# Two gate products per token become one, and the gates of the second half of the keys come back in two parts

## The reference, cut to what matters

```python
q = (hf @ w_q).reshape(T, PEER_HEADS, 2, PEER_DQ // 2)
s = jnp.einsum('thpd,hpnd->thpn', q, sub_keys)
sc, idx = lax.top_k(s, PEER_TOPK)
...
top_sc, pos = lax.top_k(cand, PEER_TOPK)
eidx = jnp.take_along_axis(cidx, pos, axis=-1)
gate = jax.nn.softmax(top_sc.astype(jnp.float32), axis=-1).astype(h.dtype)
...
act = jax.nn.gelu(jnp.einsum('thkd,td->thk', u_tab[eb], hb), approximate=False)
return jnp.einsum('thk,thkd->td', gb * act, v_tab[eb])
```

## Time and profile before

| | |
|---|---|
| median of 3 runs (lowest, highest) | 3542.27 us (3540.53, 3545.55) |
| the profiled execution | 3543.44 us |
| its span, first to last instruction | 3541.7 us |
| TensorE busy | 3341.8 us, 94% |
| VectorE busy | 2201.1 us, 62% |
| ScalarE busy | 905.8 us, 26% |
| GpSimd busy | 1880.8 us, 53% |
| DMA, mean over the span | 178 GB/s |

### The profile page before, as it was taken

One profiled execution on the slowest core, in us unless ns is written; L12 is line 12 of the kernel. 1 busy time (PEld: TensorE's weight loads), 2 busy tenths in 40 slices (PEclk: granted clock), 3 DMA queues, 4 the chain that ended last, 5 costly groups with the idle time before them and its releaser, 6 DMA issues.

```text
span 3541.7 us, 39029 instructions
## 1 busy us (share of the span) xinstructions
PE 3341.8 (94%) x14292; PEld 2517.4 (71%) x14292; DVE 2201.1 (62%) x3653; ACT 905.8 (26%) x1952; POOL 1880.8 (53%) x1072
## 2 busy tenths in 40 slices
PE   8999999999999999999999999997899988996898
PEld 5779778886857888688776677766899655663433
DVE  5764443337674333589367767899655896566765
ACT  4564431112174111201123413222211221111111
POOL 3544269997104999698775472222577333342420
PEclk9999999999999999999999999999755999998999
DMA  4430022222302222234312127777622899999996
GB/s 161 166 130 1 24 86 102 97 107 83 131 36 72 95 95 95 83 110 143 104 72 95 37 89 300 279 267 279 220 86 103 333 364 417 381 412 375 384 417 268
DMA packets 117764, 628.72 MB, mean 178 GB/s; under 512 B 12889, under 2 KB 13017, under 8 KB 62041
## 3 DMA queue, kind: packets, MB, share of 16 engines
q1 hardware_dynamic: 72496, 343.07, 26.3%
q0 software_dynamic: 36864, 268.45, 19.4%
q10 hardware_dynamic: 8232, 14.95, 1.1%
HBM read 607.55 MB, written 18.87 MB: 177 GB/s over the span
## 4 chain that ended last, share of the span: by engine, by line
PE 72%; DVE 11%; DMA 10%; issue 3%; ACT 2%; POOL 1%; DVEq 0%; ACTq 0%; POOLq 0%; SPq 0%
PE bank L1447 13%; PE bank L1448 13%; PE bank L1449 13%; PE bank L2017 6%; PE bank L2032 6%; PE bank L2044 6%; DMA residual<-in_peer_ut 5%; DMA residual<-in_peer_vd 3%; DVE arena L3549 1%; PE bank L1893 1%; PE bank L1875 1%; PE bank L1761 1%; DVE squares L3381 1%; PE bank L1394 1%; PE bank L1639 1%
## 5 line engine op out<-in xcount | busy, mean ns | idle before, releaser
L1449 PE MATMUL bank<-split_arena 128*128 128x512 f32 x1776 | 696.3, 392 | 0.0
L1279 POOL DMA_INDIRECT arena<-in_peer_uv,rstd x181 | 261.8, 1446 | 624.3 <-DVE weight_ring L3561 325.3
L1186 POOL TENSOR_TENSOR split_arena<-weight_ring,ones 128x1024 fp32r<-128x1024 f32 x204 | 505.1, 2476 | 155.1 <-PE bank L1449 99.2
L1447 PE MATMUL bank<-split_arena 128*128 128x512 f32 x1392 | 546.6, 393 | 5.4 <-DVE split_normed L2908 2.5
L1448 PE MATMUL bank<-split_arena 128*128 128x512 f32 x1392 | 542.5, 390 | 0.0
L2017 PE MATMUL bank<-normed,residual 128*128 128x256 f32 x2048 | 483.3, 392 | 55.1 <-ACT arena L2659 37.1
L1188 POOL TENSOR_TENSOR split_arena<-weight_ring,split_arena 128x1024 fp32r<-128x1024 f32 x204 | 520.1, 2550 | 16.0
L2032 PE MATMUL bank<-residual,arena 128*128 128x512 f32 x1024 | 468.7, 604 | 47.3 <-DVE arena L3537 41.4
L2017 PEld LDWEIGHTS bank<-normed,residual 128*128 128x128 f32 x2048 | 395.9, 196 | 162.0 <-issue 59.8
L2032 PEld LDWEIGHTS bank<-residual,arena 128*128 128x128 f32 x1024 | 190.4, 192 | 288.2 <-issue 238.6
L1449 PEld LDWEIGHTS bank<-split_arena 128*128 128x128 f32 x1776 | 334.4, 188 | 73.1
(11 more groups left out here) (508 smaller groups left out, 5476.9 us busy)
## 6 DMA issues: line engine op xcount, KB each, us to landing
residual<-in_peer_ut SPq DMA_DIRECT2D x128, 512.0 KB, 7.5
residual<-in_peer_vd SPq DMA_DIRECT2D x128, 512.0 KB, 11.0
weight_ring<-in_w_up SPq DMA_DIRECT2D x32, 1024.0 KB, 4.8
weight_ring<-in_w_down SPq DMA_DIRECT2D x32, 1024.0 KB, 4.8
weight_ring<-in_w_in SPq DMA_DIRECT2D x32, 1024.0 KB, 4.9
weight_ring<-in_ada_w SPq DMA_DIRECT2D x24, 1024.0 KB, 4.8
weight_ring<-in_w_in_a SPq DMA_DIRECT2D x12, 1024.0 KB, 6.6
weight_ring<-in_w_out SPq DMA_DIRECT2D x12, 1024.0 KB, 6.9
```

What stands on the lines that cost most here:

```text
L1186: pool.tensor_tensor(hi, part, bc_mid(ones[:], DT), ALU.mult).then_inc(split_hi, 1)
L1279: pool.indirect_dma_start(row_places[i][0], None, a["peer_uv"], bass.IndirectOffsetOnAxis(ap=experts[n][:, c:c + 1], axis=0)).then_inc(row ...
L1447: pe.matmul(psum[t.bank][:], hi, a_hi[k], start=first, stop=False)
L1449: return pe.matmul(psum[t.bank][:], hi, a_lo[k], start=False, stop=last)
```

## The change

- The product of a token is one of 128x128 instead of two of 128x64; the eight tokens of a step lie four in each of the two banks.
- Of the eight second one-hots of a step, VectorE makes six in one instruction, without the gate; ScalarE multiplies them by the gate (`scale_ones`, six instructions); GpSimd makes two, with the gate.
- ScalarE copies the second half from both banks in two instructions, and VectorE multiplies the first half from both banks in two, after ScalarE's copies (`gate_read`).
- The stored gates come back in two parts of 32 second keys: 64 loads of 128 KB with eight places instead of 32 of 256 KB with four. The first 40 loads are issued one behind each item's load from item 132 on; the 32 multiplications of the first part stand in the steps of items 131 to 162; the other 32 stand in 4 back steps.
- Rows per stage: 64, 24, 114, 2, 52 instead of 64, 10, 120, 2, 60.

```diff
--- before.py
+++ after.py
@@ -60,7 +60,10 @@
 WHALF = NKEY // 2
 GTOK = 8
 NGATE = DENSE // GTOK
-LOADS = 4
+LOADS = 8
+BACKS = 2
+BACK_J = WHALF // BACKS
+POOL_HOT = 2
 RAWS = 4
 RING8 = 8
 PIECES = 8
@@ -571,6 +574,8 @@
         STEPS += [("item", n) for n in range(WHALF, 3 * WHALF)]
         BACK_AT = len(STEPS)
         STEPS += [("back", i) for i in range(NGATE // LOADS)]
+        BACK_ITEM = WHALF + WHALF + 4
+        back_at = {MIX_AT + WHALF + 3 + q: q for q in range(NGATE)}
         LAST_AT = len(STEPS)
         STEPS += [("item", n) for n in range(3 * WHALF, 4 * WHALF)]
 
@@ -783,7 +788,7 @@
         one_first = [k.rearrange("p (t i) -> p t i", i=NKEY) for k in keys_t]
         one_second = [x.rearrange("p (t j) -> p t j", j=NKEY) for x in (h_tok[:, 2, :], h_tok[:, 3, :])]
         gate_out = [work_a, work_b]
-        gate_back = [k[:, i * SEQ:(i + 1) * SEQ] for k in keys_t for i in range(2)]
+        gate_back = [k[:, i * UNIT_N:(i + 1) * UNIT_N] for k in keys_t for i in range(4)]
         index_t = [masks[:, 3 * i:3 * i + 3, :] for i in range(2)]
         TAIL = W_AT + DENSE * WHALF
         iota_key = arena[:, TAIL:TAIL + NKEY]
@@ -905,6 +910,8 @@
         turn_in = sem("dense_gates_normalized")
         vector_hot = sem("vector_one_hot_ready")
         pool_hot = sem("pool_one_hot_ready")
+        scaled_hot = sem("one_hot_scaled")
+        gate_read = sem("gate_banks_copied")
         gate_stored = [sem(f"gate_half_stored{i}") for i in range(2)]
         gate_landed = [sem(f"gate_half_landed{i}") for i in range(LOADS)]
         gate_used = sem("gate_half_used")
@@ -979,7 +986,7 @@
 
         step_us = [6.1 if s < 35 else 3.6 if s < G_AT else 3.0 if s < MIX_AT else 3.5 for s in range(len(STEPS))]
         row_step = []
-        for a0, a1, rows in ((3, G_AT, 64), (G_AT, MIX_AT, 10), (MIX_AT, BACK_AT, 120), (BACK_AT, LAST_AT, 2), (LAST_AT, LAST_AT + 58, 60)):
+        for a0, a1, rows in ((3, G_AT, 64), (G_AT, MIX_AT, 24), (MIX_AT, BACK_AT, 114), (BACK_AT, LAST_AT, 2), (LAST_AT, LAST_AT + 58, 52)):
             total, at = sum(step_us[a0:a1]), 0
             ends = list(itertools.accumulate(step_us[a0:a1]))
             for i in range(rows):
@@ -1080,15 +1087,17 @@
                     sp.wait_ge(item_done, n - RAWS + 1)
                 sp.dma_start(raws[n % RAWS], a["peer_vd" if value else "peer_ut"][m]).then_inc(raw_landed[n % RAWS], 16)
 
-            def load_gates(q):
-
-                if q == 0:
+            def load_gates(n):
+
+                part, q = divmod(n, NGATE)
+                if n == 0:
                     full(sp, gate_tiles[NGATE - 1][0])
                     for x in gate_stored:
                         sp.wait_ge(x, 16 * NGATE // 2)
-                if q >= LOADS:
-                    sp.wait_ge(gate_used, q - LOADS + 1)
-                sp.dma_start(gate_back[q % LOADS], weights_dram[q]).then_inc(gate_landed[q % LOADS], 16)
+                if n >= LOADS:
+                    sp.wait_ge(gate_used, n - LOADS + 1)
+                sp.dma_start(gate_back[n % LOADS], weights_dram[q][:, part * BACK_J * GTOK:(part + 1) * BACK_J * GTOK]).then_inc(
+                    gate_landed[n % LOADS], 16)
 
             for n in range(len(ITEMS)):
                 load_item(n)
@@ -1099,11 +1108,10 @@
                 elif n == 16:
                     sp.wait_ge(half_done, 2 * (rest_units[2].u + 1))
                     sp.dma_start(y_flat[:, D:3 * D], first_units[PH - 1].src).then_inc(held_landed[0], 16)
-                elif n == 2 * WHALF:
-                    for q in range(LOADS):
-                        load_gates(q)
+                elif BACK_ITEM <= n < BACK_ITEM + NGATE + LOADS:
+                    load_gates(n - BACK_ITEM)
                 elif n == 3 * WHALF + RAWS - 1:
-                    for q in range(LOADS, NGATE):
+                    for q in range(NGATE + LOADS, BACKS * NGATE):
                         load_gates(q)
                     sp.dma_start(H[:, :, :], x_dram).then_inc(x_back, 16)
             for n in range(TT):
@@ -1288,7 +1296,7 @@
                 if q == 0:
                     for x in index_tiles:
                         have(pool, x)
-                for x in range(GTOK // 2, GTOK):
+                for x in range(GTOK - POOL_HOT, GTOK):
                     at = GTOK * t + x
                     m = pool.tensor_scalar(one_second[q % 2][:, x, :], iota_key, index_t[b][:, 1, at:at + 1],
                                            index_t[b][:, 2, at:at + 1], ALU.is_equal, ALU.mult)
@@ -2023,10 +2031,10 @@
                 if m == 0:
                     for t in v_tiles:
                         free(pe, t)
-                    for t, _ in gate_tiles[NGATE - 2:]:
+                    for t in gate_tiles[NGATE - 2] + gate_tiles[NGATE - 1]:
                         have(pe, t)
                 elif m == WHALF:
-                    pe.wait_ge(gate_used, NGATE)
+                    pe.wait_ge(gate_used, BACKS * NGATE)
                 for b in range(2):
                     for c in range(2):
                         x = pe.matmul(psum[2 * b + c][:], blk(weights[:, m % WHALF, :], b), raws[n % RAWS][:, 512 * c:512 * (c + 1)],
@@ -2037,12 +2045,13 @@
 
                 pe.wait_ge(vector_hot, q + 1)
                 pe.wait_ge(pool_hot, q + 1)
+                pe.wait_ge(scaled_hot, q + 1)
                 for t in gate_tiles[q]:
                     free(pe, t)
                 for x in range(GTOK):
-                    for half, t in enumerate(gate_tiles[q]):
-                        m = pe.matmul(psum[t.bank][:, x * WHALF:(x + 1) * WHALF], one_first[q % 2][:, x, :],
-                                      one_second[q % 2][:, x, half * WHALF:(half + 1) * WHALF], start=True, stop=True)
+                    t = gate_tiles[q][2 * x // GTOK]
+                    m = pe.matmul(blk(psum[t.bank], x % (GTOK // 2)), one_first[q % 2][:, x, :], one_second[q % 2][:, x, :],
+                                  start=True, stop=True)
                 m.then_inc(psum_full, 1)
 
             for s, (kind, v) in enumerate(STEPS):
@@ -2660,14 +2669,25 @@
 
             def keep_gates(q):
 
-                t = gate_tiles[q][1]
                 if q >= 2:
                     act.wait_ge(gate_stored[q % 2], 16 * (q // 2))
-                full(act, t)
-                act.activation(gate_out[q % 2].rearrange("p (j t) -> p j t", t=GTOK), psum[t.bank][:].rearrange("p (t j) -> p j t", t=GTOK),
-                               ACT.Copy).then_inc(bank_out[t.bank], 1)
-                have(act, t)
+                full(act, gate_tiles[q][0])
+                dst = gate_out[q % 2].rearrange("p (j t) -> p j t", t=GTOK)
+                for x, t in enumerate(gate_tiles[q]):
+                    m = act.activation(dst[:, :, x * GTOK // 2:(x + 1) * GTOK // 2],
+                                       psum[t.bank][:].rearrange("p (t j) -> p j t", j=NKEY)[:, WHALF:, :], ACT.Copy)
+                m.then_inc(gate_read, 1)
+                act.wait_ge(gate_read, q + 1)
                 act.dma_start(weights_dram[q], gate_out[q % 2]).then_inc(gate_stored[q % 2], 16)
+
+            def scale_ones(q):
+
+                b, t = divmod(q, NGATE // 2)
+                act.wait_ge(vector_hot, q + 1)
+                for x in range(GTOK - POOL_HOT):
+                    one = one_second[q % 2][:, x, :]
+                    m = act.activation(one, one, ACT.Copy, scale=index_t[b][:, 2, GTOK * t + x:GTOK * t + x + 1])
+                m.then_inc(scaled_hot, 1)
 
             def weigh_row(r):
 
@@ -2697,6 +2717,8 @@
                 if s - 1 in index_at:
                     b = index_at[s - 1]
                     take(index_tiles[b], index_t[b].rearrange("p a n -> p (a n)"), width=3 * NKEY)
+                if kind == "gate":
+                    scale_ones(v)
                 if s and STEPS[s - 1][0] == "gate":
                     keep_gates(STEPS[s - 1][1])
                 if s in exp_at:
@@ -3511,30 +3533,31 @@
                         have(dve, x)
                 dve.tensor_tensor(one_first[q % 2], bc_mid(iota_key, GTOK), bc_last(index_t[b][:, 0, GTOK * t:GTOK * (t + 1)], NKEY),
                                   ALU.is_equal)
-                for x in range(GTOK // 2):
-                    at = GTOK * t + x
-                    m = dve.tensor_scalar(one_second[q % 2][:, x, :], iota_key, index_t[b][:, 1, at:at + 1],
-                                          index_t[b][:, 2, at:at + 1], ALU.is_equal, ALU.mult)
-                m.then_inc(vector_hot, 1)
+                own = GTOK - POOL_HOT
+                dve.tensor_tensor(one_second[q % 2][:, 0:own, :], bc_mid(iota_key, own), bc_last(index_t[b][:, 1, GTOK * t:GTOK * t + own], NKEY),
+                                  ALU.is_equal).then_inc(vector_hot, 1)
 
             def gate_weights(q):
 
-                t = gate_tiles[q][0]
                 if q == 0:
                     for x in u_tiles[WHALF - 2:WHALF]:
                         have(dve, x)
```

(28 more changed lines are left out.)

## The result

The changed kernel takes 3514.14 us (median of 4 runs, 3507.12 to 3516.11) against 3542.28 us (median of 4 runs beside them): ratio 0.9916, 95% interval 0.9899 to 0.9933. The forecast was 3503, range 3478 to 3530: the median lies in the range, 11 us above the forecast. The profiled execution of after took 3507.12 us, the lowest of its four (the others 3513.57 to 3516.11), so by profiled executions the step is 36 us and by medians 28, where the forecast was 40.

The account below looks back on a forecast made before the run. The prediction took TensorE to bound the gate stage and row bytes on the DMA engines the mixed and last stages, except where VectorE does. Its terms, 5 - 8 - 5 - 20 - 12 = -40 us, gave 3503 us, range 3478 to 3530.

Parts of the forecast that it names:

- Gate stage: Gate stage: TensorE's records halve, but extra rows and waits between VectorE and ScalarE eat the saving; +5 us, bounds 0 and +30.
- The loop: Gate stage: VectorE's multiplication waits for ScalarE's scalings and copies, 2.5 us; steps of 5.26 us, 7.60 with a row.
- Rival 5: Gate stage: longer through gaps between instructions, at its upper bound, the rest as said; 3528 us, chance 0.10.
- rival 1: Gate stage: ScalarE's work is hidden behind VectorE's, so the stage takes 147 us; 3426 us in all, chance 0.05.
- Rival 3: Gate stage: two GpSimd products a step hold up VectorE's two-input instructions, 50 us slower; 3553 us, chance 0.06.
- First mixed items: First 64 mixed items: three rows fewer relieve VectorE's searches, then the DMA; -8 us, bounds 0 and -16.
- Second mixed items: Second 64 mixed items: fewer rows and no stall, against 40 smaller gate loads; -5 us, bounds -12 and +12.
- Rival 4: Second mixed items: 40 items with 1 KB-packet loads take 6.8 us instead of 3.9, +108 us; 3611 us, chance 0.03.
- the stall of four loads at once: Second mixed items: removing TensorE's stall behind the first four gate loads gives 5 us, besides 6 of idle DMA.
- Gates back: Wait before the last 64 items: fewer, smaller loads with eight in flight cut 41.3 us to 20.5; -20 us, bounds -12 and -27.
- Last items: Last 64 items: at 0.90 rows an item, rows landed in advance last for most of the stage; -12 us, bounds -5 and -16.
- Rival 2: Mixed and last stages: while any gather waits, tables go at 3.77 us, so 25 us of gains go; 3528 us, chance 0.11.

Follow-up runs that it names:

- a_oldrows: The changed kernel with the old row counts (10, 120, 2, 60 after the first 64): 3500.34 us, ratio 0.988.
- b_gate: The kernel before with the gate stage's scatter change alone, rows and gates back as before: 3508.82 us, ratio 0.9905.
- a_rowsfirst: The changed kernel with VectorE's row adds and dots put ahead of its bank multiplication in a gate step: 3459.26 us, ratio 0.9757.
- b_rows: The kernel before with the new row counts alone (24, 114, 2, 52): 3528.26 us, ratio 0.996.
- a_tied: The changed kernel with one ScalarE wait added that ties the last stage's rows to the items: 3505.45 us, ratio 0.9886.
- b_back: The kernel before with the gates back in two parts alone (128 KB loads, eight places, 40 among the items): 3533.62 us, ratio 0.9966.
- b_spread: The kernel before with its first four gate loads issued behind every fourth table instead of all at once: 3540.44 us, ratio 0.9989.
- a_both: The changed kernel with rows ahead of the bank multiplication, counts 32, 106, 2, 52, last rows tied to items over 61 steps: 3437.5 us, ratio 0.97.

## Why the prediction was right, and where not

*Gate stage: +5 said, +0.9 seen by the rows, +0.1 by the stretch that the sum covers.* The loop was right in each link: 2.46 us of idle time (2.5 said), steps of 7.56 with a row and 5.22 without (7.60, 5.26), 2.33 us for a row (2.34), by the trace, a_oldrows and b_gate. The sum of 224.4 us runs from VectorE's first one-hots to the first mixed product, and it was set against 219, which the earlier trace rows count from TensorE's first product. The first one-hots, of before and then of after:

```profile
2523.87 1.22 DVE L3512 TENSOR_TENSOR mem_keys<-arena,masks 128x1024 f32<-128x1024 f32 x1 [3.19 <-ACT masks L2143]
```

```profile
2521.10 1.23 DVE L3534 TENSOR_TENSOR mem_keys<-arena,masks 128x1024 f32<-128x1024 f32 x1 [3.18 <-ACT masks L2152]
```

The first mixed products start at 2750.23 and 2747.55, so this stretch took 226.4 us before and 226.5 after. The sum was thus 2 us low, and the +5 came of comparing two different stretches. Against 226.4 the same sum gives -2 and a forecast of 3496 us, so this slip brought the forecast 7 us nearer to the 3514 by luck. Rival 5 (gaps between instructions) is refuted with that, and rival 1 as well. One price on a side path was off: sixteen records of 128 columns took 3.75 us at the granted clock of 0.50, not 3.4.

Rival 3, GpSimd holding VectorE, is refuted where it was placed: VectorE's 1.22 and 1.28 us instructions took as long beside GpSimd's products in before as with nothing beside them in after, and at most 0.12 more in a_rowsfirst. The wait runs the other way: two products of 0.78 took 2.44 and 3.66 us. The prediction saw this and dropped it, since it was hidden. In b_rows it was not: GpSimd ended last in every fourth step, and that made the 4.7 us.

*First mixed items: -8 said, -6.5 seen* (-4.5 and -4.1 in a_rowsfirst and a_tied); b_rows gives -5.8 for the rows alone.

*Second mixed items: -5 said, -4.6 seen (-1.3 and -2.5 in those two), by two errors that cancel in part.* Three rows fewer gave 9.8 us in b_rows (7.6 said). The loads cost 8.5 in b_back and 6.3 in a_oldrows, where the terms say 13.3 - 6 - 5 = 2.3. The price of a load held (12.0 us of DMA time against 13.3). What failed is the last term, the stall of four loads at once: taken as 5 us on top of the 6 of idle DMA, while b_spread shows that stall and idle DMA are one thing, worth 4. The prediction had said that slow items would last for two or three items at the start; they came in groups through the whole stretch, ten over 4.2 us in after. Rival 4 is refuted all the same: with 6.6 us at most, and few of them, they are far from forty.

*Gates back: -20 said, -18.8 seen*, -16.9 alone in b_back. VectorE waited four times for loads in this stretch of after, 7.4 us in all, where the prediction had one wait of 7 and landings of 3.

*Last items: -12 said, -3.8 seen: the step that failed.* It took the schedule's 0.90 rows an item as the demand on the DMA engines, so that rows landed in advance would last. But no engine is held to the schedule there. Rows go as fast as they land, one per table, and the 52 rows bring the 3.76 us item whatever their rate on paper; 36 items ran at it before and 25 after, and eleven at 0.33 are 3.7 us. The prediction's own sign, 3.44 until near the end, was not there. Tied to the items the rows left 14 such items, and at 0.85 rows an item 2 (a_both). Rival 2 described this pace, for all stages; it holds in the last, and b_rows refutes it for the mixed ones. Why the first 23 items of after run at TensorE's pace is open. Four tables are in flight, and TensorE's other work there (one item of 7.06 us, three of 4.31) lets them get ahead; but with 60 rows, in before, the fast start ends after 19 items, so the rows have a part in it. This was not tested.

*The range and the total.* By medians the change brought 28 us instead of 40, and 8 of the missing 12 are the last stage. The stated range does not follow from the bounds of the parts: added as independent, by squares, they give 3489 to 3536, which holds the median too. And rival 4's forty items at 6.8 instead of 3.9 are 116 us, not 108.

*What was not asked.* The prediction gave the cost of the 14 rows in the gate stage (33 us) and what they bring elsewhere, but in different sums. Put side by side, 2.34 a row against 8 + 7.6 + 12 = 27.6 for 14 rows, 2.0 each, it would have said by itself that this part of the change loses. And the 2.5 us of idle VectorE in each step, named as what is late next, were the room in which a row costs nothing.

The Trainium skill (SBUF — State Buffer, Who interferes with whom) lets whichever of VectorE and GpSimd comes first block the other. In the earlier trace rows GpSimd comes first, at 2708.50, and its first product takes 0.79 us, as alone; VectorE's two-input addition starts inside it, at 2709.04, and takes 1.28 us, as alone. GpSimd's second product, which starts after that addition, takes 2.76. In the step of a_rowsfirst above GpSimd's 3.66 us are one product of 2.87, begun 0.14 us after VectorE's addition, and one of 0.80. So these runs show the block in one direction, and in the other at most 0.12 us.

## What to carry to other kernels

When an in-order engine waits for another one in every step of a loop, put independent work of its own between what it hands over and what it waits for: here 54 us for the order of two calls, and eight more rows for 0.1 us. When a sum is set against a row, check that both begin and end at the same instruction. Before moving work between stages, price a unit in both by the same measure, what ends last there. In a stage bound by the DMA engines a compute stall is worth only the DMA time it wastes; and a rate written in a schedule is a rate only where some wait ties the work to it.
